# A hybrid decoder step on one core: the embedding norm's gain and bias move to the transposes' readout, the decode tokens finish inside the last matmul stage

## What is computed

```python
xp = _layer_norm(concat([meta, x_prompt]), ln_emb_g, ln_emb_b)   # embedding norm
proj = x @ w_in + b_in                                           # q, f, v, gate, u
o_hg  = gated linear recurrence over q, k = 1-f, v, with a decay f
o_ssm = complex diagonal state space over u (S5), then a GLU
x   = _layer_norm(ALPHA * x + concat([o_hg, o_ssm]) @ w_out, ln1_g, ln1_b)
ffn = _peer(x, w_q, keys, u_tab, v_tab)    # top 16 of 128*128 experts, 8 heads
x   = _layer_norm(ALPHA * x + ffn, ln2_g, ln2_b)
```

## Time and profile before

| | us |
|---|---|
| runs shown, median (lowest to highest) | 1132.56 (1132.36 to 1134.69) |
| the profiled execution, its own time | 1134.14 |
| its span | 1132.3 |
| PE busy | 1072.6 |
| DVE busy | 860.9 |
| POOL busy | 603.5 |
| ACT busy | 545.7 |

### The profile page before, as it was taken

How to read it: one execution, slowest core, us unless ns; L and a number is a source line. 1 busy time by engine, 2 the same in 40 slices (tenths; PEclk the granted TensorE clock), 3 DMA queues, 4 the chain that set the end, 5 groups by cost and what they waited for, 6 DMA issues and landing times.

```text
span 1132.3 us, 21255 instructions
## 1 busy us (share of the span) xinstructions
PE 1072.6 (95%) x6906; PEld 935.1 (83%) x6906; DVE 860.9 (76%) x1970; ACT 545.7 (48%) x1102; POOL 603.5 (53%) x557
## 2 busy tenths in 40 slices
PE   3999987998999999899999999999999999999994
PEld 2785477646989999899999999998788888888882
DVE  5926893542899999949999999926677776777767
ACT  2151031203557777665545444455555555555552
POOL 3992582205659999789999999882010110101101
PEclk9999998898999999999999999999999999999997
DMA  8340126406335555456666666648877767777651
GB/s 291 97 150 1 74 75 171 126 0 220 127 120 170 192 179 182 167 187 226 210 212 211 211 209 206 203 167 286 312 238 245 251 227 250 229 248 252 226 201 42
DMA packets 73647, 209.30 MB, mean 185 GB/s; under 512 B 11056, under 2 KB 20400, under 8 KB 73472
## 3 DMA queue, kind: packets, MB, share of 16 engines
q1 hardware_dynamic: 64384, 175.20, 44.9%
q0 software_dynamic: 9216, 33.56, 10.5%
HBM read 202.23 MB, written 4.73 MB: 183 GB/s over the span
## 4 chain that ended last, share of the span: by engine, by line
PE 72%; POOL 12%; DVE 8%; issue 5%; DMA 2%; ACT 1%; POOLq 0%; SPq 0%; DVEq 0%; ACTq 0%
PE bank L830 30%; PE bank L750 27%; POOL parts L1625 6%; PE bank L813 5%; PE bank L733 4%; PE bank L570 1%; PE bank L769 1%; PE bank L716 1%; PE bank L706 1%; DMA raw<-in_blocks 1%; DVE q_dec L1258 1%; DVE pre L1271 1%; DVE small L1077 1%; DMA rows_emb<-in_rows 1%; PE bank L627 1%
## 5 line engine op out<-in xcount | busy, mean ns | idle before, releaser
L865 ACT ACTIVATE parts<-raw 128x512 fp32r<-128x512 f32 x544 | 343.1, 632 | 349.8 <-PE bank L750 203.6
L1625 POOL TENSOR_TENSOR parts<-raw,parts 128x512 fp32r<-128x512 f32 x292 | 383.4, 1332 | 119.4 <-ACT parts L865 114.5
L750 PE MATMUL bank<-xw,parts 128*128 128x256 f32 (+1 forms) x3456 | 437.2, 287 | 6.4 <-POOL parts L1625 4.3
L750 PEld LDWEIGHTS bank<-xw,parts 128*128 128x128 f32 x3456 | 424.0, 191 | 7.8 <-POOL parts L1625 4.6
L830 PE MATMUL bank<-parts,w_hi 128*128 128x512 f32 x1024 | 315.6, 389 | 0.7 <-DVE w_lo L1489 0.7
L1481 DVE TENSOR_TENSOR parts<-raw,parts 128x512 fp32r<-128x512 f32 x252 | 171.6, 692 | 96.2 <-ACT parts L865 95.3
L830 PEld LDWEIGHTS bank<-parts,w_hi 128*128 128x128 f32 x1024 | 192.2, 188 | 40.8 <-DVE parts L1481 1.1
L830 PE MATMUL bank<-parts,w_lo 128*128 128x512 f32 x512 | 199.3, 389 | 0.0
L1660 POOL DMA_INDIRECT v_got<-in_blocks,row_u x32 | 35.8, 1119 | 272.1 <-DVE acc_s L1510 264.3
L830 PEld LDWEIGHTS bank<-parts,w_lo 128*128 128x128 f32 x512 | 96.2, 188 | 19.8
L1439 DVE TENSOR_SCALAR hot_g<-bank,idx_t 128x128 f32<-128x128 f32 x256 | 101.3, 396 | 0.0
(11 more groups left out here) (295 smaller groups left out, 1091.6 us busy)
## 6 DMA issues: line engine op xcount, KB each, us to landing
raw<-in_blocks SPq DMA_DIRECT2D x272, 512.0 KB, 3.4
w_ring<-in_w_in SPq DMA_DIRECT2D x5, 2048.0 KB, 8.2
w_ring<-in_w_out SPq DMA_DIRECT2D x2, 2048.0 KB, 7.7
s_samp<-in_state SPq DMA_DIRECT2D x8, 256.0 KB, 6.1
rows_ln<-in_rows SPq DMA_DIRECT2D x4, 512.0 KB, 6.2
out_hg_sample<-s_samp SPq DMA_DIRECT2D x8, 256.0 KB, 5.5
rows_emb<-in_rows SPq DMA_DIRECT2D x2, 512.0 KB, 6.5
wglu<-in_w_glu SPq DMA_DIRECT2D x1, 1024.0 KB, 5.4
```

The costliest lines, as they stand in the source:

```text
L750: last = mm(b[:, 0:cols], w[:, a, :], xw[:, x, c, 0:cols], start=(c == 0 and (a, x) == (0, 0)), stop=(c == DC - 1 and a == 1))
L865: A(parts[:, q % 4, 0, :], raw[:, s % 4, (q % 2) * 512:(q % 2 + 1) * 512], ACT.Copy).then_inc(hi_ready, 1)
L1625: G.tensor_tensor(parts[:, q % 4, 1, :], raw[:, q // 2 % 4, (q % 2) * 512:(q % 2 + 1) * 512], parts[:, q % 4, 0, :].bitcast(F32), ALU.subt ...
```

## The change

Four edits, made together.

1. **Order of loads.** All of x is issued first, then weight group 0, `cols`, `s5raw`, weight group 1, the masks, and only then `rows_emb`. ACT's queue issues the three constants. `lane` grows by 16 columns: the embedding norm's gain and bias by channel.
2. **Embedding norm.** DVE's `standardize` takes x less its mean times the reciprocal, in one tensor_scalar; gain and bias are applied by channel where the transposes are read out of PSUM (`embed`), four pieces a bank, by ACT and for the last bank by DVE. Since x itself is wanted again at the first residual, DVE multiplies and adds `rows_emb` to it later, six operations behind the memset of `suf`.
3. **Decode tokens.** A row is added behind every third block of v, from block 2 on; PE sums them after block 103 (`SUM_AT = 104`), and DVE finishes their norm behind block 105, with ACT's square root in the same place.
4. **Tail.** The last two blocks of v wait for all of their parts and run by tile of tokens, so that tile 0's banks are full first; tile 1's last operation is split in halves, each sent out by itself; ACT and POOL finish tile 0 alone.

```diff
@@ SP
-            for i in range(2):
-                sp.dma_start(rows_emb[:, i, :], rows_in[i, :].partition_broadcast(P)).then_inc(rows_sem, 16)
...
-            sp.dma_start(ident[:, :], consts_in[:, 0:P]).then_inc(consts_sem, 16)
...
             load_w(0)
+            sp.dma_start(cols[:, :], cols_in).then_inc(cols_sem, 16)
...
+            load_w(1)
             sp.dma_start(mask_words[:, :], masks_in).then_inc(masks_sem, 16)
-            load_w(1)
+            for i in range(2):
+                sp.dma_start(rows_emb[:, i, :], rows_in[i, :].partition_broadcast(P)).then_inc(rows_sem, 16)
@@ shared
+        def embed(op, eng, t, halves=(0, 1)):
...
+                for k in range(4):
+                    c = 4 * i + k
+                    dst, src = x_t[:, c, t0:t0 + n], bank_of("xT", t, i)[:, k * n:(k + 1) * n]
+                    g, b = emb_g[:, c:c + 1], emb_b[:, c:c + 1]
+                    if eng is nc.scalar:
+                        last = op(dst, src, ACT.Identity, scale=g, bias=b)
+                    else:
+                        last = op(dst, src, g, b, ALU.mult, ALU.add)
@@ PE
-            with pe.Fori(1, NK // 2, 1) as i:
+            with pe.Fori(1, SUM_AT // 2, 1) as i:
...
             pe.wait_ge(v_added, NG)
             for half in range(2):
...
+                last = mm(bank[0][NG * half:NG * half + NG, :], sel_s[:, :], acc_s[:, half * 512:(half + 1) * 512],
+                          start=True, stop=True, tile_position=(0, NG * half))
+            last.then_inc(ys_full, 1)
+            with pe.Fori(SUM_AT // 2, NK // 2 - 1, 1) as i:
...
+            pe.wait_ge(wlo_ready, NK)
+            pe.wait_ge(lo_ready, V_HALF + 2 * NK)
+            for t in range(2):
+                for s in range(2):
+                    for half in range(2):
...
+                last.then_inc(y_full, 1)
@@ ACT
+            act.wait_ge(consts_sem, 48)
+            for t in range(3):
+                deviation(0, t)
+                if t > 0:
+                    embed(A, act, t - 1)
+            embed(A, act, 2, (0,))
...
+            deviation(2, 2, NG, turn=0)
+            with act.Fori(SUM_AT // 4, NK // 4 - 1, 1) as i:
+                v_round(i)
@@ DVE
+            def standardize(t):
...
+                dve.wait_ge(ln_std, t + 1)
+                link(V.reciprocal(rstd[:n, 3 + t:4 + t], rstd[:n, 3 + t:4 + t]))
+                V.tensor_scalar(x, x, mv[:n, 2 * t:2 * t + 1], rstd[:n, 3 + t:4 + t], ALU.subtract,
+                                ALU.mult).then_inc(x0_ready, 1)
...
+                statistics(x_tok[:TILES[t][1], t, :], t, TILES[t][1])
+                if t > 0:
+                    standardize(t - 1)
+            standardize(2)
+            dve.wait_ge(consts_sem, 48)
+            embed(V.tensor_scalar, dve, 2, (1,))
...
+            dve.wait_ge(rows_sem, 32)
+            computed(dve, "xT", 2, 1)
+            for t, (t0, n) in enumerate(TILES):
+                link(V.tensor_tensor(x_tok[:n, t, :], x_tok[:n, t, :], rows_emb[:n, 0, :], ALU.mult))
+                link(V.tensor_tensor(x_tok[:n, t, :], x_tok[:n, t, :], rows_emb[:n, 1, :], ALU.add))
...
+            for n in range(2, NK):
+                low_part(V_ROUND, 2 * n)
+                low_part(V_ROUND, 2 * n + 1)
+                w_low(0, n)
+                if n % 3 == 2 and n // 3 < NG:
+                    add_row(n // 3)
+                if n == SUM_AT + 1:
+                    dve.wait_ge(ys_full, 1)
...
+                    layer_norm(x_s[0:NG, :], 2, NG, rows_ln2, 2, rows2_sem, y_sample_ready, turn=0)
@@ POOL
-            for t in range(2):
-                pool.wait_ge(scaled, t + 1)
-                G.tensor_tensor(x_res[:, t, :], x_res[:, t, :], rows_ln2[:, 1, :], ALU.add).then_inc(y_out_ready, 1)
+            pool.wait_ge(scaled, 1)
+            G.tensor_tensor(x_res[:, 0, :], x_res[:, 0, :], rows_ln2[:, 1, :], ALU.add).then_inc(y_out_ready, 1)
```

More of the change, by code:

```diff
@@ L50 @@
 G_ROUND = U_ROUND + G_FIRST // 4
+SUM_AT = 104
 V_ROWS = (QB + NK) * NK
@@ L405, in trunk @@
         a_bar = (ar, ai)
+        emb_g, emb_b = lane[:, 9:9 + DC], lane[:, 9 + DC:9 + 2 * DC]
+        def embed(op, eng, t, halves=(0, 1)):
+            t0, n = TILES[t]
+            for i in halves:
+                computed(eng, "xT", t, i)
+                for k in range(4):
[6 more added lines that the diff above has]
+                        last = op(dst, src, g, b, ALU.mult, ALU.add)
+                readout(last, "xT", t, i)
         block = ctx.enter_context(nc.Block())
@@ L1061, in _ @@
                 w_high(NK // 4 - 1, s)
[L1062 to L1066, removed]
+            deviation(2, 0, P, turn=1)
+            act.wait_ge(centred, 1)
+            A(x_res[:, 0, :], x_res[:, 0, :], ACT.Copy, scale=rstd[:, 3:4]).then_inc(scaled, 1)
+            deviation(2, 1, P, turn=2)
         @block.vector
@@ L1072, in _, with statistics @@
             V = dve
-            def layer_norm(x, t, n, rows, k, rows_landed, ready, shared=False):
+            def statistics(x, t, n):
                 for i in range(2):
@@ L1081, in layer_norm @@
                                 ALU.add).then_inc(ln_var, 1)
+            def layer_norm(x, t, n, rows, k, rows_landed, ready, shared=False, turn=None, pieces=1):
+                statistics(x, t, n)
                 dve.wait_ge(rows_landed, 32)
                 link(V.scalar_tensor_tensor(x, x, mv[:n, 2 * t:2 * t + 1], rows[:n, 0, :], ALU.subtract, ALU.mult))
-                dve.wait_ge(ln_std, 3 * k + t + 1)
+                dve.wait_ge(ln_std, 3 * k + (t if turn is None else turn) + 1)
                 if shared:
@@ L1498, in _, with add_row @@
             dve.wait_ge(c_ready, 1)
[L1499 to L1507, removed]
-                else:
-                    dve.wait_ge(v_added, n)
-                    V.scalar_tensor_tensor(acc_s[:, :], v_got[k][:, :], c_s[:, n:n + 1], acc_s[:, :], ALU.mult,
+            def add_row(k):
+                dve.wait_ge(v_row[k % 4], 16 * (k // 4 + 1))
+                if k == 0:
+                    V.tensor_scalar(acc_s[:, :], v_got[0][:, :], c_s[:, 0:1], None, ALU.mult).then_inc(v_added, 1)
+                else:
+                    dve.wait_ge(v_added, k)
+                    V.scalar_tensor_tensor(acc_s[:, :], v_got[k % 4][:, :], c_s[:, k:k + 1], acc_s[:, :], ALU.mult,
```

85 lines of the change are left out of this document (45 added, 40 removed).

## The result

| | before | after |
|---|---|---|
| median of 6 runs, us | 1133.43 | 1143.44 |
| lowest to highest | 1132.36 to 1135.37 | 1139.19 to 1146.84 |
| the profiled execution, its own time | 1134.14 | 1139.19 |
| its span | 1132.3 | 1137.4 |
| PE busy | 1072.6 | 1077.4 |

The change makes the kernel slower: 1.0084 times the time before, 95% interval 1.0067 to 1.0100, some 10 us. That is the side that was forecast, at more than double the size, and above the range. The profiled execution of after happens to be the shortest of its six; what it lacks is shown further down by a second profile of the same kernel (e12).

What follows compares the result with a forecast made beforehand. PE held 72% of the chain, POOL bounding 28 to 93 us and DVE the tail. Terms -4.6 + 6.0 + 2.4 + 3.8 + 1.5 - 0.75 - 4.5 = +3.85 on median 1132.56 gave 1136.4 us, range 1130.0 to 1139.4.

Steps and rivals of the forecast that it cites:

- The head, what is won: Head: the last readout into x_t moves from 21.99 to 17.4 us, 4.6 won, up to 6.3 without memset collision.
- Rival (4): Head: x not there sooner, tile 1 at 8 or later, 3 won: 1138.0 us; shares chance 0.43 with the forecast.
- The head, what is paid: POOL's ladder: six DVE operations on x_tok cost POOL 1.0 us each, 6.0 paid, between 0 and 7.3.
- The reading of L1593: POOL operation beside a DVE one: 1.88 us against 1.25 alone, read as losing just DVE's streaming time, 0.63.
- Rival (2): Ladder and memset: the port shared by DVE and POOL costs nothing, 1128.7 us; chance 0.13.
- The v stage: Block 3: DVE stands for row 0's fetch, so PE waits; 2.4 us paid, between 1.5 and 4.0.
- the other 31 rows fit DVE's idle quarter: nothing: v stage: the remaining rows, every 8.1 us instead of 10.9, fit DVE's idle time and cost nothing.
- Sums and norm: Behind block 103: PE's sums and DVE's decode-token norm delay block 106; 3.8 us paid, between 3.0 and 4.2.
- One fall for the two pauses: v stage: PE's pauses before blocks 3 and 106 bring one clock fall, 1.5 us, between 0 and 3.0.
- Rival (3): v stage: the clock falls at all three pauses, the last two blocks' too, 3.0 us more: 1139.4; chance 0.16.
- A pause of 1.75 us, but tile 0 has its banks 0.75 before: Last two blocks: PE waits 1.75 us for w_lo, yet tile 0's banks come 0.75 us sooner, won.
- The tail: From DVE's first read to the last issue 10.75 us against 15.57; 4.5 won after 0.3 for later landing.

Runs made afterwards that it cites:

- e12: The kernel after the change, unchanged, measured and profiled once more: 1146.89 us.
- e8: After, with the added rows three blocks later and POOL's third memset behind the norm of all three tiles: 1138.72 us, ratio 1.0047.
- e5: e4 with the six x_tok operations moved into DVE's wait for the second chunk state, rows_emb loaded ahead of the z_t transfers: 1131.35 us, ratio 0.9979.
- e1: Before with only the new order of loads and the new embedding norm: 1139.67 us, ratio 1.0040.
- e4: After with row 0 added behind block 5 instead of block 2, the others three blocks later each: 1138.65 us, ratio 1.0044.
- e6: e4 with the decode tokens' norm in five pieces behind blocks 105, 106, 108, 110 and 112, ACT's square root a round later: 1133.99 us, ratio 1.0011.
- e7: e4 with the last pair of blocks waiting for each block's parts as they come: 1135.74 us, ratio 1.0018.
- e2: Before with only the decode-token and tail edits: 1140.60 us, ratio 1.0059.
- e3: After with the six x_tok operations moved into DVE's wait for the second chunk state, rows_emb loaded behind the writes of z_t: 1143.00 us, ratio 1.0092.

## Why the prediction was wrong, step by step

- **"The head, what is won" (4.6): 2.98.** The collision with the memset came as taken (tile 0 ready at 10.85 for 11.0); DVE's operation took 2.16 us, ended 0.54 behind the memset's end, and takes 0.81 without the memset (e8). The Trainium skill's rule ("SBUF — State Buffer", Who interferes with whom), that a DVE operation in a two-port mode and a GpSimd one exclude each other for the whole instruction, agrees with that. Tile 1 was in time, and PE's transposes too (15.4 for 15.6). What was mis-sized is ACT's piece: 0.25 us was read off two 192-column copies, and pieces with scale and bias by channel follow each other at 0.34. ACT works without a break from 12.13 to 18.98 at twenty of them and a root of 0.2; at 0.25 that is 5.2 us, and it would have ended at 17.3. Rival (4), x not there sooner, is not what happened, though it gives the same size.
- **"The head, what is paid" (6.0): 6.05.** Right in size, and e5 shows the cause. The reading of L1593 was right in effect only: POOL does not lose DVE's streaming time, it gets through one operation per DVE operation, so the loss is the distance between these less its own length. By six whole lengths it would be 7.3; the trace shows less, because DVE's next operation starts 1.26 us behind the last although POOL's 0.25 lies between. Rival (2) falls.
- **Missing: PE's wait before the first levels, the largest step that failed.** The text follows POOL's chain to the scan, says that PE's projections lie beside it, and puts nothing for what PE does between the scan and the v stage. It never asked what happens when the projections end earlier and the scan later. PE's cover before was thin (0.82 us idle); 6.08 us of idle brought a fall, 1.7 us. From the scan to block 0 of the v stage the delay grows by 3.7 us in the second profile, 4.0 in e1, 1.7 to 2.0 in e4, e6 and e7; in the first profile the lucky search hides it.
- **"The v stage", row 0 (2.4, of 1.5 to 4.0): 1.8 in the first profile, 3.9 in the second with its fall.** Right. The wait before block 20, 1.2 to 1.3 us more than in before, was not in it: "the other 31 rows fit DVE's idle quarter: nothing" looked at DVE, not at the transfers: a fetch every 8.1 us instead of 10.9, while x_res and rows_ln2 are loaded too. That this traffic is what delayed the raw block is argued, not shown: the wait is gone in e4, but in e2, with the same earlier rows, it is gone too.
- **Sums and norm (3.8, of 3.0 to 4.2): 1.1 and 2.6,** 3.7 without the fall. Right.
- **"One fall for the two pauses" (1.5, of 0 to 3.0): the step that failed in the v stage.** Both profiles of after have a fall ahead of the levels and two in the v stage (block 106 in both, the pair in the first, block 3 in the second), 1.7 us each: 3.4 for 1.5 in the v stage alone. Rival (3) had falls at all three pauses of the v stage, at 0.16. The row it was weighed with, 1.05 us of idle in 3 that left the clock alone, was a single example of another length.
- **"A pause of 1.75 us, but tile 0 has its banks 0.75 before": 1.78, and 1.0 later** in the first profile, since the fall stretched the pair. In the second, without a fall there, DVE's first read comes 17.33 us later than before where the blocks stand 17.9 later, 0.6 sooner: the netting was right, the fall was not in it. That the pause need not be paid at all the text did not see; e7 shows 2.9 us to be had there, the fall included.
- **"The tail" (10.75 from first read to last issue): 10.86.** Right.

In sum, by the second profile: 3.4 at the scan, 3.7 more by the v stage (2.3 by 166 us, with the fall before the levels; 1.6 from 189 to 267, where the clock is at half from 202.9 to 216.6 against 199.3 to 209.5 in before; 0.6 behind 486, half for 6.9 us against 3.4; less 0.9 around 180), 5.2 up to block 21, 1.2 for the sums, 4.3 for the norm and its fall, 2.1 at the pair: 20.0 us at PE's last matmul, less 7.2 behind it, 12.8. That is 8.9 above the forecast's +3.85: 2.0 at the scan (3.4 for the +1.4 that the head was to cost), 3.7 from there to the v stage and 1.3 at block 20, which both stood at nothing, and 1.9 for the falls in the v stage (3.4 for 1.5). The median of after, 10.0 above before, lies between the two profiles. The forecast had the right parts and both signs; it lost by taking three things as too small: what follows a pause, ACT's piece, and PE's thin cover before the levels.

## What to carry to other kernels

A pause of PE is priced with the half-speed stretch that may follow it, each pause with its own, and a pause far from the change counts as soon as the change moves its two sides apart. A free engine is no free place: ask which engine shares the port with it and whether that one is on the path. When a step is put into a stage without idle time, cut it into small pieces (e6), and start its loads a few blocks ahead (e4); the same edits then gave 0.992 in place of 1.008.

## What was not expected of the hardware

- Beside DVE operations of 1.23 us in a chain, POOL's operations of 0.24 us took 1.17 to 1.30, one per DVE operation; where both had long ones (e3), both stretched: DVE's from 1.23 to 1.95, POOL's eight from 9.43 to 14.40. The Trainium skill ("SBUF — State Buffer", SBUF: two separate sides) lets whoever starts first keep the shared port pair for the whole instruction, and counts in a DVE operation with two SBUF inputs when the GpSimd one reads SBUF. Here POOL's small operations come near to that: each ends 0.1 us behind a DVE operation; but whole turns would set DVE's 1.48 us apart (1.23 and 0.25), and they are 1.26. In e3 whole turns would set DVE's 2.4 us apart (1.23, and 9.43 / 8 for one of POOL's), and they are 1.99. No run here says how the two were interleaved.
- PE's idle time of 1.5 to 2.5 us was followed by a half clock in some executions and not in others, of one kernel too: behind 1.78 us at the pair in the first profile of after and in e4, not in the second; behind 2.44 us at block 106 in both profiles of after and in e3, but not in e2, e4, e5, e7 and e8.
- DVE's operations on `tk_eq` that start while a POOL addition runs end 0.55 us behind its end (1.64 to 1.79 us for 0.69), the casts on `tk_abf` 0.05 behind it (1.15 to 1.20 for 0.20): the shorter the operation, the larger its loss beside its own length. Since ACT meets the end of the search at a fixed place of its order, a few short operations more or less that meet an addition set two executions of one kernel 5 us apart.
